# Sharing the first head's 32-block inverse between VectorE and GpSimd, and asking for it three slots earlier

## The chip, the cores and the metric

The kernel runs on one core of one Trainium2 chip. The metric is the device time of one launch in microseconds (us), the median of several runs. Before the change three runs gave 2298.82, 2300.39 and 2301.43 us, median 2300.39 us.

## The reference

A decoder trunk of two layers over 1024 tokens of width 1024. Layer 0 is a gated DeltaNet with 8 heads (key width 128, value width 256), layer 1 a dilated sliding-window attention. Each layer is an RMS norm, one input projection, the mixer, a gate, an output projection and a residual add. The part that matters here is the triangular solve of the delta rule:

```
lower = where(strict, einsum("bhnid,bhnjd->bhnij", k_beta, k) * decay, 0.0)
rhs   = concatenate([v * beta, k_beta * exp(g)], axis=-1)
sol   = triangular_solve(lower + eye(C), rhs, left_side=True, lower=True, unit_diagonal=True)
```

The kernel solves it by inverting unit lower triangular matrices, for 8 tiles of 128 tokens in each head.

## The kernel before, in words

Everything is one program with five instruction queues (TensorE = PE, VectorE = DVE, ScalarE = ACT, GpSimd = POOL, SyncE = SP), each in program order, tied together by counting semaphores. There is no scheduler: the order on each queue is written out by hand in **slots**. One head of the delta layer has 36 slots (0 to 35) and trails of up to 42. In every slot TensorE does 8 matmuls of 128x512 of the input projection (`three_passes`, L383): 6 weight units of 128 columns a head, each in two halves of 512 tokens, a half q = 0..11 in slots 3q to 3q+2. Weights are split in a high and a low part, so a half takes 24 matmuls. Around these matmuls stand the other steps of the head, each in a fixed slot.

`body(m, n, p)` writes one round: it projects head n and, beside it, runs the delta recurrence of the head before, m. The first round has no m. So the first head's inverse is made in the round `body(None, 0, 0)` and used in the next, `body(0, 1, 1)`, from slot 4 on.

**The inverse.** The tiles u (the strictly lower matrices) are written to DRAM in slot 16 (L658) and their 32x32 diagonal blocks come back as `bd`, one block a partition spread over four partition groups (L663). Each group q of 32 partitions computes 8 of the 32 columns of the inverse of its blocks: `bx` is 128 partitions x 32 rows x 8 columns. GpSimd does a forward substitution in 31 steps: step j multiplies column j of `bd` below the diagonal by row j of `bx` (L766, into `bt`) and subtracts the product from the rows below (L769). Each of the 62 instructions waits on a semaphore for the one before. At last a copy turns `bx` (L774, into `bxt`, which lies in `bd`).

**The way back.** In slot 33 (INVERSE_BACK) the SP queue waits for that copy, stores four parts of `bx` and four of the turned copy (L711, L712), waits for them, and issues four loads into `zx` (L716). TensorE reads `zx` in slot 4 of the next round (L1112), from which two levels build the 128-inverse (L1112, ScalarE's copy L823, L1117 and L1119).

**Weights.** In every slot s with s mod 6 = 3 the SP queue issues one weight load of 512 KB (L620; unit j = s//6 + 1, and in slot 33 unit 0 of the next head), once its buffer is free, which is when VectorE's low part of the unit before the last is done (`wa_w_low`). ScalarE makes the high part (L786) one slot ahead of VectorE's low part (L1128). The two buffers alternate. In the code, slot 33's weight load stands ahead of slot 33's inverse wait.

**Evacuation and gates.** ScalarE copies each finished half out of PSUM in slot 3q+3 (L864 for q below 8, L872 for the last four) and runs three passes for its sigmoid in slot 3q+5 (L877, L879, L881). VectorE does the four taps of the convolution and the sigmoid's argument in slot 3q+4 (L1258, L1260, L1266) and the product with the sigmoid in slot 3q+6 (L1273, or L1277 for the gate halves). TensorE's half q in slot 3q waits until ScalarE has evacuated half q-2. TensorE turns the value halves 4 to 7 in slots 20, 23, 26 and 29 (L1057), for which it waits until VectorE has made them (L1273), and multiplies keys with queries in slots 21 and 24 (L1091); the second of these waits for VectorE's use of the first (L1299). The keys are turned in slots 32 and 35 (L1049).

Of the kernel before, what the change touches and what calls it, by code (L numbers as in the profile page):

```python
# [22 lines left out]
ALU = mybir.AluOpType  # L23
# [21 lines left out]
BLK = 32  # L45
NB = P // BLK
LEVELS = 2
PARTS_OF_BLOCK = P // BLK
PART = BLK // PARTS_OF_BLOCK
# [11 lines left out]
def spread(ap, axis, n):  # L61

    v = ap.unsqueeze(axis)
    shape = list(v.shape)
    shape[axis] = n
    return v.broadcast_to(shape)


class Mem:
# [11 lines left out]
    def sem(self, name):  # L81
        return self.ctx.enter_context(self.nc.semaphore(f"{self.tag}_{name}"))
# [278 lines left out]
Q_GRAMS = (21, 24)  # L361
BLOCKS_OUT = 16
INVERSE_BACK = 33
DELAYED = SLOTS + 6
OUT_RING = 8
OUT_TILES = A_VW // P
# [59 lines left out]
def delta_heads(nc, g, weights, proj, o_turned, front, o_stored, early):  # L426
# [5 lines left out]
    with ExitStack() as ctx:  # L432
# [17 lines left out]
        cols = m_.sb("cols", [P, 7, T, H])  # L450
        hc = m_.sb("hc", [P, 2, 6, T])
        hw = m_.sb("hw", [P, 2, CONV, 4])
        bd = m_.sb("bd", [P, BLK, BLK])
        bx = m_.sb("bx", [P, BLK, PART])
# [7 lines left out]
        r = m_.sb("r", [P, DV])  # L462
# [8 lines left out]
        rows = m_.sb("rows", [4 * H, HALF], F32R)  # L471
# [33 lines left out]
        sem = m_.sem  # L505
# [12 lines left out]
        blocks_out, blocks_in, blocks_inv = sem("blocks_out"), sem("blocks_in"), sem("blocks_inv")  # L518
        inv_out, inv_zero = sem("inv_out"), sem("inv_zero")
        back = [sem("back_first"), sem("back_rest")]  # L520
        bstep = sem("bstep")
        zx_zero = sem("zx_zero")
        um_s, first_mm, first_c, lv_mm, lv_s = (sem(x) for x in ("um", "first_mm", "first_c", "lv_mm", "lv_s"))
        ks_mm, r_s, xr_mm, vn_s = sem("ks_mm"), sem("r_s"), sem("xr_mm"), sem("vn_s")
# [90 lines left out]
        def _(sp):  # L615
# [21 lines left out]
            def body(m, n, p):  # L637
                for s in range(DELAYED):
                    if n is not None and s < SLOTS and s % 6 == 3:
                        j = s // 6 + 1  # L640
# [60 lines left out]
                    if m is not None and (s - CHAIN0 - 8) % 3 == 0 and 0 <= (s - CHAIN0 - 8) // 3 < T:  # L701
                        t = (s - CHAIN0 - 8) // 3
                        sp.wait_ge(og_s, m * T + (t + 1 + T))
                        dst = o_turned[bass.ds(m * DV, DV), t * P:(t + 1) * P].rearrange("(c p) n -> p c n", p=P)
                        sp.dma_start(dst, og[:, :, :]).then_inc(o_stored, 16)
                    if n is not None and s == INVERSE_BACK:
                        sp.wait_ge(blocks_inv, n * 2 + 2)

                        sp.wait_ge(lv_s, n * (LEVELS * T // 2) + 1)
                        for q in range(PARTS_OF_BLOCK):  # L710
                            sp.dma_start(as_blocks(inv_dram[1])[:, :, columns(q)], part_of(bx, q)).then_inc(inv_out, 16)  # L711
                            sp.dma_start(as_blocks(inv_dram[0])[:, columns(q)], part_of(bxt, q)).then_inc(inv_out, 16)  # L712
                        sp.wait_ge(inv_out, (n + 1) * (32 * PARTS_OF_BLOCK))
                        for part, tiles in enumerate((slice(0, 2), slice(2, T))):
                            for c in range(2):
                                sp.dma_start(zx[:, tiles, c, :], as_tiles(inv_dram[c])[:, tiles]  # L716
                                             ).then_inc(back[part], 16)
# [3 lines left out]
        @block.gpsimd  # L721
        def _(pool):
            pool.memset(zx[:, :, :, :], 0.0).then_inc(zx_zero, 1)
            pool.wait_ge(cols_s, 1)

            def body(m, n, p):
                if n is not None:
                    columns_and_taps(n, p)
                if m is not None:
                    for b in range(T // 2):  # L730

                        pool.wait_ge(first_mm, m * (LEVELS * T // 2) + (LEVELS * max(b - 1, 0) + 1))
                        pool.wait_ge(ut, m * 4 + 2)
                        pool.tensor_tensor(um[:, b % 2], spread(u[:, 2 * b:2 * b + 2, :], 2, LEVELS),  # L734
                                           spread(g.level_mask[:, :, :], 1, 2), ALU.mult).then_inc(um_s, 1)
                if n is not None:
                    invert_blocks(n)

            def columns_and_taps(n, p):

                pool.wait_ge(og_s, n * T)
                pool.tensor_copy(hc[:, p], cols[:, 0:C_LOG, :, bass.ds(n, 1)].rearrange("p a t o -> p a (t o)")
                                 ).then_inc(hc_s, 1)
                pool.tensor_copy(pick[:, p, :], cols[0:4 * H, C_LOG, 0:2, bass.ds(n, 1)].rearrange("r a o -> r (a o)")
                                 ).then_inc(hc_s, 1)
                for c, tile in ((0, n + H), (1, n + 0), (2, n * 2 + 2 * H), (3, n * 2 + (2 * H + 1))):
                    pool.tensor_copy(hw[:, p, :, c:c + 1], g.conv[:, :, bass.ds(tile, 1)]).then_inc(hc_s, 1)

            def invert_blocks(n):

                if not (isinstance(n, int) and n == 0):
                    pool.wait_ge(inv_out, n * (32 * PARTS_OF_BLOCK))
                pool.sem_inc(carrier, 1)
                pool.memset(bx[:, :, :], 0.0).then_inc(bstep, 1)
                pool.wait_ge(bstep, n * (2 * BLK) + 1)
                pool.sem_inc(carrier, 1)
                for q in range(PARTS_OF_BLOCK):
                    diag = part_of(bx, q)[:, columns(q), :].rearrange("t i c -> t (i c)")[:, 0:PART * PART:PART + 1]
                    ins = pool.tensor_copy(diag, part_of(g.ones, q)[:, 0:PART])
                ins.then_inc(bstep, 1)  # L760
                pool.wait_ge(blocks_in, (n + 1) * (16 * PARTS_OF_BLOCK))
                for j in range(BLK - 1):
                    pool.wait_ge(bstep, n * (2 * BLK) + (2 + 2 * j))
                    rows, width = BLK - 1 - j, min(j + 1, PART)
                    prod = bt[:, 0:rows * width].rearrange("t (i c) -> t i c", c=width)
                    pool.tensor_tensor(prod, spread(bd[:, j, j + 1:BLK], 2, width),  # L766
                                       spread(bx[:, j, 0:width], 1, rows), ALU.mult).then_inc(bstep, 1)
                    pool.wait_ge(bstep, n * (2 * BLK) + (3 + 2 * j))
                    pool.tensor_tensor(bx[:, j + 1:BLK, 0:width], bx[:, j + 1:BLK, 0:width], prod,  # L769
                                       ALU.subtract).then_inc(bstep if j < BLK - 2 else blocks_inv, 1)  # L770

                pool.wait_ge(blocks_inv, n * 2 + 1)
                pool.sem_inc(carrier, 1)
                pool.tensor_copy(bxt, bx[:, :, :].rearrange("t i c -> t c i")).then_inc(blocks_inv, 1)  # L774
                pool.wait_ge(blocks_inv, n * 2 + 2)
                pool.sem_inc(bstep, 1)

            heads(pool, body)
# [346 lines left out]
        def _(dve):  # L1125
# [50 lines left out]
            def next_weight(n, s):  # L1176
                j = s // 6 + 1
                if j < UNITS or n < H - 1:
                    split_low(n * UNITS + (1 + j), slot_of(j % UNITS))

            def body(m, n, p):
                pm = 1 - p
                for s in range(DELAYED):
                    if m is not None:
                        b, k = divmod(s - LEVEL0 - 2, LEVEL_STEP)
                        if 0 <= b < T // 2 and k in range(0, 2 * LEVELS, 2) and not (n is not None and s == CHAIN0 + 1):
                            merge(m, b, k // 2)
                        t, k = divmod(s - CHAIN0, 3)
# [19 lines left out]
                        t, k = divmod(s - CHAIN0 - 6, 3)  # L1208
# [5 lines left out]
                    if n is not None:  # L1214
                        if s - 1 in K_GRAMS:
# [7 lines left out]
                            for e in range(TH):  # L1223
                                t = half * TH + e
# [44 lines left out]
                        if 0 <= q < HALVES and k == 0:  # L1269
# [4 lines left out]
                            else:  # L1274
                                c = q // 2 - 4
# [1267 lines left out]
```

## Time and profile before

| | us |
|---|---|
| three runs | 2298.82, 2300.39, 2301.43 |
| the profiled execution's own time | 2299.51 |
| its span, first to last instruction | 2297.8 |
| PE busy | 2243.4 (98%) |
| DVE busy | 1400.1 (61%) |
| ACT busy | 1229.9 (54%) |
| POOL busy | 400.2 (17%) |

Times in the rows are microseconds from the span's start. The first head's round runs from about 44 to 123 us: the turn of its last keys in slot 35 starts at 122.95 us, and the first matmul of the second head's slot 0 at 123.31 us. An instruction's row gives its start, its duration, engine, line, operation, tiles and shapes, and in brackets how long its engine sat idle before it and what released it.

### The profile page before, as it was taken

The numbers are of one execution on the slowest core, as the hardware profiler recorded it, in microseconds if no ns is written. First come the engines' busy times: TensorE is split into PE (matmuls) and PEld (weight loads), VectorE is DVE, ScalarE is ACT, GpSimd is POOL, SyncE is SP. The second block draws the span as 40 slices with busy tenths as digits, with TensorE's granted clock in tenths as the row PEclk, the third lists the DMA queues.
The fourth block names the chain that finished last, engine by engine and source line by source line (L and its number), as shares of the span: only waits on it lengthen the run. The fifth ranks groups of instructions, "written<-read, shape, count | busy, mean of one in ns | idle before, by whom it ended". The sixth has DMA issues, their size and how long they took to land. (4 is left out here: it accounts for less than half of the span.)

```text
span 2297.8 us, 31341 instructions
## 1 busy us (share of the span) xinstructions
PE 2243.4 (98%) x11056; PEld 1873.0 (82%) x11056; DVE 1400.1 (61%) x2594; ACT 1229.9 (54%) x2509; POOL 400.2 (17%) x672
## 2 busy tenths in 40 slices
PE   7989999999999999999999999999999999999989
PEld 5778888887888888787888888888888888888877
DVE  5756767585767665586745728365482745738341
ACT  5646566666666665555545455454554545455430
POOL 1435161533425160560000000000000000000000
PEclk9999999999999999999999999999999999999999
DMA  4222232313222245585111121121111211121151
GB/s 142 46 53 62 63 88 51 81 41 75 49 67 60 58 104 179 183 273 192 56 38 56 28 59 44 38 65 38 47 37 47 65 38 56 28 56 47 54 217 51
DMA packets 301727, 174.26 MB, mean 76 GB/s; under 512 B 97229, under 2 KB 284005, under 8 KB 301573
## 3 DMA queue, kind: packets, MB, share of 16 engines
q1 hardware_dynamic: 301572, 172.26, 26.3%
q8 instruction: 90, 1.47, 0.3%
q14 instruction: 65, 0.52, 0.1%
HBM read 143.66 MB, written 28.56 MB: 75 GB/s over the span
## 5 line engine op out<-in xcount | busy, mean ns | idle before, releaser
L383 PE MATMUL b_front<-g_h_hi,wa_w_hi 128*128 128x512 f32 x2064 | 822.5, 398 | 4.7 <-PEq L1503 3.0
L383 PE MATMUL b_front<-g_h_lo,wa_w_hi 128*128 128x512 f32 x2064 | 827.0, 401 | 0.0
L383 PE MATMUL b_front<-g_h_hi,wa_w_lo 128*128 128x512 f32 x2064 | 823.4, 399 | 0.0
L383 PEld LDWEIGHTS b_front<-g_h_hi,wa_w_hi 128*128 128x128 f32 x2064 | 389.1, 189 | 81.5 <-issue 5.5
L383 PEld LDWEIGHTS b_front<-g_h_lo,wa_w_hi 128*128 128x128 f32 x2064 | 388.9, 188 | 77.1 <-issue 0.2
L383 PEld LDWEIGHTS b_front<-g_h_hi,wa_w_lo 128*128 128x128 f32 x2064 | 388.6, 188 | 76.1 <-issue 0.5
L2154 ACT ACTIVATE b_acc<-b_front,g_gains 128x512 f32<-128x512 f32 x96 | 66.1, 689 | 301.7 <-DVE b_qk L2458 211.2
L1260 DVE SCALAR_TENSOR_TENSOR a_acc<-a_x_raw,a_hw,a_acc 128x512 f32<-128x512 f32 x192 | 156.9, 817 | 6.8
L2332 DVE TENSOR_TENSOR wa_w_lo<-wa_raw,wa_w_hi 128x1024 fp32r<-128x1024 f32 x79 | 95.6, 1210 | 106.0 <-ACT wa_w_hi L2100 106.0
L766 POOL TENSOR_TENSOR a_bt<-a_bd,a_bx 128x112 f32<-128x112 f32 (+29 forms) x248 | 117.3, 473 | 214.8 <-DMA a_bd<-u_tiles 196.0
L769 POOL TENSOR_TENSOR a_bx<-a_bx,a_bt 128x112 f32<-128x112 f32 (+29 forms) x248 | 130.6, 527 | 19.4
L2423 DVE TENSOR_TENSOR b_sq_lo<-b_sg,b_sq_hi 128x512 fp32r<-128x512 f32 x96 | 66.3, 690 | 89.4 <-ACT b_sq_hi L2159 89.4
L877 ACT ACTIVATE a_sg<-a_sg 128x512 f32<-128x512 f32 x96 | 60.0, 625 | 78.6 <-DVE a_sg L1266 78.6
L2458 DVE TENSOR_TENSOR b_qk<-b_acc,b_sg 128x512 f32<-128x512 f32 x96 | 90.2, 939 | 0.0
L2187 ACT ACTIVATE b_v<-b_side 128x512 f32<-128x512 f32 x48 | 28.6, 595 | 106.8 <-PE b_side L2315 106.8
L2015 DVE COPY b_kept<-b_ring 128x512 f32<-128x512 f32 (+1 forms) x28 | 18.3, 653 | 107.3 <-PE b_ring L2264 107.3
L2100 ACT ACTIVATE wa_w_hi<-wa_raw 128x1024 fp32r<-128x1024 f32 x79 | 82.7, 1047 | 0.0
L734 POOL TENSOR_TENSOR a_um<-a_u,g_level_mask 128x512 f32<-128x512 f32 x32 | 42.2, 1327 | 229.4 <-PE a_lev L1112 229.2
L2166 ACT ACTIVATE b_v_raw<-b_front 128x512 f32<-128x512 f32 x48 | 28.6, 595 | 90.6 <-PE b_front L383 90.6
L2243 PE MATMUL b_ring<-b_qk 128*128 128x128 f32 (+1 forms) x384 | 76.6, 322 | 0.0
L830 ACT ACTIVATE a_o<-a_step,a_hc 128x256 f32<-128x256 f32 x56 | 26.6, 475 | 90.9 <-DVE a_r L1191 90.9
L1128 DVE TENSOR_TENSOR wa_w_lo<-wa_raw,wa_w_hi 128x1024 fp32r<-128x1024 f32 x47 | 58.4, 1243 | 23.4 <-ACT wa_w_hi L786 23.4
(343 smaller groups left out, 4087.0 us busy)
## 6 DMA issues: line engine op xcount, KB each, us to landing
wa_raw<-in_b_w_in_dram SPq DMA_DIRECT2D x80, 512.0 KB, 3.9
wa_raw<-in_a_w_in_dram SPq DMA_DIRECT2D x48, 512.0 KB, 4.3
p_w_raw<-in_a_w_out_dram SPq DMA_DIRECT2D x40, 512.0 KB, 3.9
a_out<-a_og SPq DMA_DIRECT2D x64, 128.0 KB, 1.9
a_zx<-inverse_tiles SPq DMA_DIRECT2D x16, 384.0 KB, 4.5
p_a_raw<-a_out SPq DMA_DIRECT2D x40, 128.0 KB, 5.0
u_tiles<-a_u SPq DMA_DIRECT2D x8, 512.0 KB, 3.2
a_bd<-u_tiles SPq DMA_DIRECT2D x32, 128.0 KB, 3.7
```

What stands on the lines that cost most here:

```text
L383: last = pe.matmul(out, w[:, k, :], a[:, k, ks], start=(n == 0), stop=(n == 23))
L766: pool.tensor_tensor(prod, spread(bd[:, j, j + 1:BLK], 2, width), spread(bx[:, j, 0:width], 1, rows), ALU.mult).then_inc(bstep, 1)
L769: pool.tensor_tensor(bx[:, j + 1:BLK, 0:width], bx[:, j + 1:BLK, 0:width], prod, ALU.subtract).then_inc(bstep if j < BLK - 2 else blocks_i ...
L877: act.activation(sg[:, q % 2], sg[:, q % 2], ACT.Exp).then_inc(sigs, 1)
L1128: dve.tensor_tensor(w_lo[slot][:, :, :], raw[:, slot], w_hi[slot][:, :, :].bitcast(F32), ALU.subtract).then_inc(w_low, 1)
L1260: ins = dve.scalar_tensor_tensor(acc[:, half], src, w, acc[:, half], ALU.mult, ALU.add)
L2100: act.activation(w_hi[slot_of(j)][:, :, :], raw[:, slot_of(j)], ACT.Copy).then_inc(w_high, 1)
L2154: act.activation(acc[:, half], proj[half][:, :], ACT.Copy, scale=r.gains[:, gain:gain + 1]).then_inc(rope, 1)
L2243: mm = pe.matmul(ring[i % 3][:, c * 2 * P:c * 2 * P + width], qk[:, 2 * g, first:first + P], qk[:, 2 * g + 1, begin:begin + width], start= ...
L2332: dve.tensor_tensor(w_lo[slot_of(j)][:, :, :], raw[:, slot_of(j)], w_hi[slot_of(j)][:, :, :].bitcast(F32), ALU.subtract).then_inc(w_low, 1)
L2423: dve.tensor_tensor(sq_lo[:, :], sg[:, q % 2], sq_hi[:, :].bitcast(F32), ALU.subtract).then_inc(sq_low, 1)
L2458: dve.tensor_tensor(out, a, b_, ALU.mult).then_inc(qkn, 1)
```

## The change

Three edits, all of them for the first head only (n = 0).

1. GpSimd's 31 steps work on columns 0 to 3 of each part (width 4 in place of 8).
2. VectorE does columns 4 to 7: 27 steps (j = 4 to 30) of two instructions, three steps at the head of each of the slots 20 to 28, with a semaphore of their own (`shared`), each instruction waiting for the one before. They use `r` as the place of the product. The columns don't depend on each other, so neither engine waits for the other's steps; GpSimd's copy L774 now waits for both.
3. The SP queue waits for the inverse and sends it to DRAM and back in slot 30 in place of 33.

```diff
+FIRST_BACK = 30
+SHARED = PART // 2
+SHARED_STEPS = {20 + i: range(SHARED + 3 * i, min(SHARED + 3 * i + 3, BLK - 1)) for i in range(9)}
...
-                    if n is not None and s == INVERSE_BACK:
+                    if n is not None and s == (INVERSE_BACK if n else FIRST_BACK):
...
-                    rows, width = BLK - 1 - j, min(j + 1, PART)
+                    rows, width = BLK - 1 - j, min(j + 1, PART if n else SHARED)
...
+                if n == 0:
+                    pool.wait_ge(shared, 2 * (BLK - 1 - SHARED))
...
+            def invert_columns(steps):
+
+                for j in steps:
+                    done = 2 * (j - SHARED)
+                    if j == SHARED:
+                        dve.wait_ge(bstep, 2)
+                        dve.wait_ge(blocks_in, 16 * PARTS_OF_BLOCK)
+                    else:
+                        dve.wait_ge(shared, done)
+                    rows, width = BLK - 1 - j, min(j + 1, PART) - SHARED
+                    cols = slice(SHARED, SHARED + width)
+                    prod = r[:, 0:rows * width].rearrange("t (i c) -> t i c", c=width)
+                    dve.tensor_tensor(prod, spread(bd[:, j, j + 1:BLK], 2, width), spread(bx[:, j, cols], 1, rows),
+                                      ALU.mult).then_inc(shared, 1)
+                    dve.wait_ge(shared, done + 1)
+                    dve.tensor_tensor(bx[:, j + 1:BLK, cols], bx[:, j + 1:BLK, cols], prod, ALU.subtract
+                                      ).then_inc(shared, 1)
+
             def body(m, n, p):
                 pm = 1 - p
                 for s in range(DELAYED):
+                    if m is None and s in SHARED_STEPS:
+                        invert_columns(SHARED_STEPS[s])
```

The diff doesn't show what edit 3 moves on the SP queue, because slots 30 and 33 lie in one loop. This is the queue of the kernel before, from the load of the blocks `bd` on; the three weight loads in its second row are units 4 and 5 of the first head (slots 21 and 27) and unit 0 of the second (slot 33).

```order
L663 DMA a_bd<-u_tiles 32x32x32 x4
L620 DMA wa_raw<-in_a_w_in_dram 128x8x128 x3
L711 DMA inverse_tiles<-a_bx 32x32x8
L712 DMA inverse_tiles<-a_bd 32x8x32
L711 DMA inverse_tiles<-a_bx 32x32x8
L712 DMA inverse_tiles<-a_bd 32x8x32
L711 DMA inverse_tiles<-a_bx 32x32x8
L712 DMA inverse_tiles<-a_bd 32x8x32
L711 DMA inverse_tiles<-a_bx 32x32x8
L712 DMA inverse_tiles<-a_bd 32x8x32
L716 DMA a_zx<-inverse_tiles 128x2x128 x2
L716 DMA a_zx<-inverse_tiles 128x6x128 x2
```

Behind these rows the queue goes on with L620 x3. And this is the same place in the changed kernel, where the lines have moved by 3.

```order
L666 DMA a_bd<-u_tiles 32x32x32 x4
L623 DMA wa_raw<-in_a_w_in_dram 128x8x128 x2
L714 DMA inverse_tiles<-a_bx 32x32x8
L715 DMA inverse_tiles<-a_bd 32x8x32
L714 DMA inverse_tiles<-a_bx 32x32x8
L715 DMA inverse_tiles<-a_bd 32x8x32
L714 DMA inverse_tiles<-a_bx 32x32x8
L715 DMA inverse_tiles<-a_bd 32x8x32
L714 DMA inverse_tiles<-a_bx 32x32x8
L715 DMA inverse_tiles<-a_bd 32x8x32
L719 DMA a_zx<-inverse_tiles 128x2x128 x2
L719 DMA a_zx<-inverse_tiles 128x6x128 x2
```

Two weight loads stand ahead of the wait where three stood, and L623 x4 follow in place of three: the second head's unit 0 has changed sides.

On VectorE, this is what stands from the sigmoid's argument of half 5 (slot 19) to the convolution of half 6 (slot 22) in the kernel before.

```order
L1266 TENSOR_SCALAR a_sg<-a_acc 128x512 [waits a_convs]
L1128 TENSOR_TENSOR wa_w_lo<-wa_raw,wa_w_hi 128x1024 [waits wa_w_high]
L1273 TENSOR_TENSOR a_acc<-a_acc,a_sg 128x512 [waits a_sig]
L1258 TENSOR_SCALAR a_acc<-a_x_raw,a_hw 128x512 [waits a_v_turned,a_evac,a_act_out]
L1260 SCALAR_TENSOR_TENSOR a_acc<-a_x_raw,a_hw,a_acc 128x512 [waits a_taps] x3
```

In the changed kernel 12 new instructions stand ahead of the weight's low part (slots 20 and 21; the last two of them are shown) and 6 ahead of the convolution (slot 22).

```order
L1198 TENSOR_TENSOR a_r<-a_bd,a_bx 128x88 [waits a_shared]
L1201 TENSOR_TENSOR a_bx<-a_bx,a_r 128x22x4 [waits a_shared]
L1133 TENSOR_TENSOR wa_w_lo<-wa_raw,wa_w_hi 128x1024 [waits wa_w_high]
L1298 TENSOR_TENSOR a_acc<-a_acc,a_sg 128x512 [waits a_sig]
L1198 TENSOR_TENSOR a_r<-a_bd,a_bx 128x84 [waits a_shared]
L1201 TENSOR_TENSOR a_bx<-a_bx,a_r 128x21x4 [waits a_shared]
L1198 TENSOR_TENSOR a_r<-a_bd,a_bx 128x80 [waits a_shared]
L1201 TENSOR_TENSOR a_bx<-a_bx,a_r 128x20x4 [waits a_shared]
L1198 TENSOR_TENSOR a_r<-a_bd,a_bx 128x76 [waits a_shared]
L1201 TENSOR_TENSOR a_bx<-a_bx,a_r 128x19x4 [waits a_shared]
L1283 TENSOR_SCALAR a_acc<-a_x_raw,a_hw 128x512 [waits a_v_turned,a_evac,a_act_out]
```

The same goes on up to slot 28, 54 new instructions in all, with every older instruction in its old order.

## Rows read from the trace of the kernel before

**Rows 1.** The page, part 1: busy time of each engine.
```profile
PE 2243.4 (98%) x11056; PEld 1873.0 (82%) x11056; DVE 1400.1 (61%) x2594; ACT 1229.9 (54%) x2509; POOL 400.2 (17%) x672
```

**Rows 2.** TensorE's waits from 40 to 200 us: engine, line, releaser, total, times, longest.
```profile
PE a_lev L1117 <- ACT a_bc L823: 4.5, 1, 4.5
...
PE a_lev L1112 <- issue: 1.7, 1, 1.7
```

**Rows 3.** TensorE in order of time, 123 to 145 us.
```profile
123.31 0.48 PE L383 MATMUL b_front<-g_h_hi,wa_w_hi 128*128 128x512 f32 x1
...
134.33 0.68 PE L1112 MATMUL a_lev<-a_zx,a_um 128*128 128x128 f32 x4 [1.68 <-issue]
...
141.31 0.80 PE L1117 MATMUL a_lev<-a_zx,a_bc 128*128 128x128 f32 x2 [4.45 <-ACT a_bc L823]
...
143.04 0.78 PE L383 MATMUL b_front<-g_h_hi,wa_w_hi 128*128 128x512 f32 x1
```

**Rows 4.** ScalarE in order of time.
```profile
112.80 1.06 ACT L786 ACTIVATE wa_w_hi<-wa_raw 128x1024 fp32r<-128x1024 f32 x1
...
117.24 0.60 ACT L872 ACTIVATE a_acc<-b_front 128x512 f32<-128x512 f32 x1 [1.54 <-PE b_front L383]
120.69 0.63 ACT L877 ACTIVATE a_sg<-a_sg 128x512 f32<-128x512 f32 x1 [2.85 <-DVE a_sg L1266]
...
139.44 1.06 ACT L786 ACTIVATE wa_w_hi<-wa_raw 128x1024 fp32r<-128x1024 f32 x1 [12.17 <-DMA wa_raw<-in_a_w_in_dram]
140.41 0.58 ACT L864 ACTIVATE a_x_raw<-b_front 128x512 f32<-128x512 f32 x1
```

**Rows 5.** The SP queue: its wait for the inverse, then its DMAs in time.
```profile
SPq L711 <- POOL a_bd L774: 31.2, 1, 31.2
...
94.25 0.37 SPq L620 DMA_DIRECT2D wa_raw<-in_a_w_in_dram  x1
...
133.58 2.17 SPq L620 DMA_DIRECT2D wa_raw<-in_a_w_in_dram  x2
```

**Rows 6.** Granted clock and busy times, 140 to 145 us.
```profile
140.00:145.00 5.00, 3.69 (x14) 3.31 (x14) 4.33 (x7) 1.26 (x3) 0.00 (x0) 0.66 0.42 113
```

**Rows 7.** GpSimd in order of time: first and last steps and some between.
```profile
87.77 0.24 POOL L766 TENSOR_TENSOR a_bt<-a_bd,a_bx 128x31 f32<-128x31 f32 x1 [34.90 <-DMA a_bd<-u_tiles]
...
93.16 1.32 POOL L769 TENSOR_TENSOR a_bx<-a_bx,a_bt 128x135 f32<-128x135 f32 x1
...
111.35 0.39 POOL L766 TENSOR_TENSOR a_bt<-a_bd,a_bx 128x120 f32<-128x120 f32 x1
111.82 0.44 POOL L769 TENSOR_TENSOR a_bx<-a_bx,a_bt 128x120 f32<-128x120 f32 x1
...
124.14 0.20 POOL L766 TENSOR_TENSOR a_bt<-a_bd,a_bx 128x8 f32<-128x8 f32 x1
...
125.17 0.67 POOL L774 COPY a_bd<-a_bx 128x256 f32<-128x256 f32 x1 [0.17 <-POOL a_bx L769]
```

**Rows 8.** Stretches: length, then busy (x) of PE, PEld, DVE, ACT, POOL; clock, DMA.
```profile
92.70:109.90 17.20, 17.20 (x89) 14.54 (x88) 14.77 (x19) 9.56 (x16) 15.55 (x22) 1.00 0.11 30
```

**Rows 9.** VectorE in order of time: the weight's low part; the first tap alone, then beside GpSimd.
```profile
89.38 0.49 DVE L1258 TENSOR_SCALAR a_acc<-a_x_raw,a_hw 128x512 f32<-128x512 f32 x1
...
92.72 1.44 DVE L1128 TENSOR_TENSOR wa_w_lo<-wa_raw,wa_w_hi 128x1024 fp32r<-128x1024 f32 x1
...
95.50 0.73 DVE L1258 TENSOR_SCALAR a_acc<-a_x_raw,a_hw 128x512 f32<-128x512 f32 x1
```

**Rows 10.** VectorE's groups by shape: mean ns of one; idle before, over the count.
```profile
L2365 DVE TENSOR_TENSOR b_mo<-b_mo,b_mx 128x8 f32<-128x8 f32 x8 | 1.3, 168 | 0.3
L2438 DVE TENSOR_TENSOR b_acc<-b_acc,t_cos 32x512 f32<-32x512 f32 x96 | 64.6, 673 | 0.0
```

**Rows 11.** TensorE's last turn of values (slot 29).
```profile
111.13 0.60 PE L1057 MATMUL a_turn<-g_ident,a_acc 128*128 128x128 f32 x4
```

**Rows 12.** The weight loads L620, 80 to 200 us: time from issue to landing.
```profile
DMA to landing us min/median/max: 4.0/5.8/6.9
```

More of the change, by code:

```diff
@@ L520, in delta_heads @@
         back = [sem("back_first"), sem("back_rest")]
-        bstep = sem("bstep")
+        bstep, shared = sem("bstep"), sem("shared")
         zx_zero = sem("zx_zero")
```

## The prediction

> **What bounds the kernel now.** I read the busy times first: TensorE is busy 98% of the span, no other engine more than 61% [rows 1]. An edit to VectorE and GpSimd can win only where TensorE stands still, so I went to TensorE's waits around the first head. Between 40 and 200 us there are two that hang on the inverse [rows 2], and the timeline shows where. In slot 4 of the second head L1112 stands idle 1.68 us for `zx`; one slot on, L1117 stands idle 4.45 us for ScalarE's copy L823 [rows 3]. Together 6.1 us.
>
> The first ends right after `zx` begins to land. The second isn't a wait for the inverse itself. ScalarE stood 12.17 us for a weight load before 139.44 (unit 1 of the second head), and L823 is queued behind that [rows 4]. The SP queue says why the load was late: SP waited 31.2 us for GpSimd's copy L774, sent the inverse away and back, and only at 133.58 issued the weight [rows 5]. So both stalls are one: the inverse ends at 125.84 (125.17 + 0.67) [rows 7], and everything behind SP's wait is late. A last cost is the clock: in 140 to 145 us the granted clock is 0.66 [rows 6], a mix of 2.4 and 1.2 GHz, after those 4.45 us idle.
>
> **Edit 1, GpSimd on half the columns.** With no collision, 120 elements take 0.39 us in the multiplication and 0.44 in the subtraction, 8 elements 0.20, and the next one starts 0.08 us behind the end of the one before [rows 7]. That is 0.19 us fixed and 0.08 idle for each instruction, 0.54 us a step, and 1.7 + 2.1 = 3.8 ns an element for the pair. The 31 steps had 2964 elements an instruction (31, 60, 87, 112, 135, 156, 175, then 8 x 24 down to 8 x 1) and get 1802 (31, 60, 87, then 4 x 28 down to 4 x 1). Undisturbed, 31 x 0.54 + 2964 x 0.0038 = 28.0 us becomes 23.6 us. Real were 37.2 us (87.77 to 125.0): 9.2 us are lost beside VectorE. One row shows how: the subtraction at 93.16 took 1.32 us while VectorE's 1024-element subtraction ran from 92.72 to 94.16, and that one took 1.44 [rows 7, 9]. Most of this loss stays, since VectorE's old instructions all stay in the stretch; I take 7.5 us. GpSimd then ends at 87.8 + 23.6 + 7.5 = 118.9 at the earliest, and the new small VectorE instructions come on top, perhaps 1 to 4 us.
>
> **Edit 2, VectorE does the other half.** 54 instructions, each waiting for the one before. No such instruction is in this place yet; the nearest are 128x8 at 168 ns with about 0.04 us idle between, and a two-input 512 one at 673 ns [rows 10], so 0.16 us + 1.01 ns an element, + 0.04. Elements are 27, 52, 75, then 4 x 24 down to 4 x 1: 1354, twice 2708. Sum: 54 x 0.20 + 2708 x 0.00101 = 13.5 us. The low end is 54 x 0.205 = 11.1 us, the elements free. For the high end each has to wait for a GpSimd instruction, as the first tap did that took 0.73 us beside GpSimd and 0.49 alone [rows 9]: 54 x 0.24 = 13 more, 26.5 us. GpSimd's instructions will be short, so I add 0.03 us each: 15.1 us.
>
> What cover is there? From 92.7 to 109.9 us VectorE is busy 14.8 of 17.2 us [rows 8]; only 2.4 us are free, and six sevenths of the new work doesn't fit. VectorE becomes the bound of this stretch. Counted out: it has 14.2 us of old work between 92.7 and its instruction behind the last new one (14.8 less the 0.6 of that instruction itself), so the last new step ends at 92.7 + 14.2 + 15.1 = 122.0. GpSimd, at 120 to 123, is close beside. The copy L774 adds 0.15 + 0.67: the inverse is ready at about **122.8** instead of 125.84, 3.0 us earlier, not 15.
>
> On the way TensorE is held. Slot 24's product waits for L1299, which comes behind 18 new instructions (about 5.5 us), and slot 29's turn of half 7 comes behind L1273, now past the steps of slots 20 to 27. That L1273 ends at about 120.6 us (122.0 less the last block's 1.4), where the turn stood at 111.13 [rows 11]. So TensorE is about 9.5 us late at slot 30. That alone would bring its slot 36 (slot 0 of the second head) from 123.31 to 132.8. It is hidden only because something still later follows.
>
> **Edit 3, the wait moved to slot 30.** It is moved past one DMA: the load of the second head's unit 0, which before was issued at 94.25 and whose high part ScalarE made at 112.80 with no wait [rows 4, 5]. Now it is issued after the inverse's trip. From L774's end to the next weight load that trip took 133.58 - 125.84 = 7.74 us; the weight issued there was waited for until 139.44, 5.86 us [rows 4, 5]. Behind ScalarE's wait for it are queued, in order: L786 itself (0.97 us to the next start), three passes of half 9's sigmoid (0.63 each, 1.96 with the gaps), and the evacuation of half 10 (0.60) [rows 4], for which TensorE's slot 36 waits. Sum 7.74 + 5.86 + 0.97 + 1.96 + 0.60 = 17.1 us. Slot 36 therefore starts at 122.8 + 17.1 = **139.9**, where it started at 123.31: 16.6 us late, and 7.1 us behind even the held TensorE.
>
> Then the gains. `zx` is there at about 131.3 (122.8 + 8.5, the time from 125.84 to the row of L1112), and unit 1's weight was issued with unit 0's: both old stalls go, 6.1 us. The restart after the 4.45 us cost (1 - 0.66) x 5 = 1.7 us [rows 6]; I count 1.0 of it before 143.04, an estimate, since the group from 141.31 to 143.04 took 1.73 us [rows 3] and is twice that of L1112 (0.68 with its tail), and 0.7 after it. Slots 36 to 41 (123.31 to 143.04) are then 19.7 - 6.1 - 1.0 = 12.6 us of work. A restart after 7 us idle pays the 1.7 again. So slot 42 begins at 139.9 + 12.6 + 1.7 = 154.2, against 143.04 + 0.7 = 143.7 before: **+10.5 us**. As a formula, the shift is the inverse's end less 112.3 us. Behind it TensorE is the bound as before, nothing gives the time back, and the other heads are unchanged.
>
> The profiled execution took 2299.51 us, 0.88 below the median of the runs. Added to the median: 2300.4 + 10.5 = **2310.9 us**.
>
> A rule of the Trainium skill speaks against this change harder than I do. SBUF — State Buffer, section "Who interferes with whom", says that a VectorE instruction with two SBUF inputs and a GpSimd instruction that reads SBUF exclude each other, and the loser is blocked until the other ends. The 1.32 us row agrees with it; the result it would give is the first rival.
>
> **Rivals.**
> *The two engines take turns.* Each of the 54 instructions waits for a running GpSimd one and the other way round. For it: 0.49 to 0.73 us, and the 1.32 us. Against it: GpSimd's waits are for long VectorE instructions, and its own are 0.2 to 0.4 us. Priced: 5 to 11 us more, inverse at 128 to 134, +16 to +22 us, about 2319.
>
> *Little changes.* The inverse comes early, at about 120, and the landing is short: the fastest of these loads land after 4.0 us [rows 12], 1.9 less, and the clock doesn't fall. +7.7 - 1.9 - 1.7 = +4.1 us, 2304.5. For it, the low bound of the new instructions.
>
> *Faster, the intended way.* The steps of both engines are done by slot 28 or 29 and the unit 0 load isn't late. It decides at an inverse's end of 112.3; full gain is below 106.2, where slot 36 starts at 123.3 and slot 42 at 135.9, 7.8 us off at most. Against it: GpSimd even undisturbed ends at 87.8 + 23.6 + 0.8 = 112.2, and VectorE would need its 15 us in 2.4. With the short landing and no slow clock that gives -0.1 - 3.6 = -3.7, 2296.7.
>
> *The change doesn't do what it says*, that is VectorE's steps wait for GpSimd's: excluded, they wait only for the blocks and the first two GpSimd steps, done long before.
>
> **How the numbers follow.** Forecast (inverse at 119 to 127, +7 to +15) 0.68; taking turns 0.18; little change 0.09; faster 0.05. One comparison of this kernel can tell 0.2%, 4.6 us. Faster by more 0.05, within 0.08, slower 0.87. The range goes from 2304.5, the little change's own time, to 2320, which takes in half of taking turns. That leaves out about 0.18: 0.05 for faster, 0.04 of the little change, 0.09 of taking turns.
>
> **What would show it.** In the changed profile: the 54 small instructions with a mean of 0.21 to 0.25 us and starts 0.26 to 0.31 us apart; L1299's successor late by 5 us; TensorE idle before the turn of slot 29 (4 to 6 us) and again before slot 0 of the second head (about 7 us, released by ScalarE's evacuation); ScalarE idle over 10 us before the high part of unit 0; the SP's wait for the copy ending near 123; no wait at L1117. I am wrong if the copy ends before 115, or if slot 36 starts before 132.

## The result: 0.44% slower, and the profile after

| | before | changed |
|---|---|---|
| median of 6 runs each, us | 2300.89 | 2310.85 |
| lowest to highest | 2298.82 to 2301.82 | 2308.34 to 2313.78 |
| ratio, 95% interval | | 1.0044, 1.0034 to 1.0054 |
| profiled execution, span | 2299.51, 2297.8 | 2311.55, 2309.8 |

The change costs 10.0 us. 2310.9 was forecast.

One thing has to be set aside before rows are compared. The delta layer's first matmul starts at 36.77 us in this profile and at 34.74 in that of before. Over all the profiled executions below, it starts anywhere from 34.3 to 37.0. So I take 2.03 us off a time of the changed kernel to set it beside one of before ("in before's time"). For a whole run's shift in a profile I take a **marker**: the start of the first `a_new<-a_v_front` matmul (slot 8 of the second head, the first place at which all kernels do the same work again) less the start of the delta layer's first matmul. It is 117.31 us in the profile of before.

The page's first part, against [rows 1]: VectorE has 54 instructions and 13.8 us more, GpSimd 8.3 us less.

```profile
PE 2248.8 (97%) x11056; PEld 1876.4 (81%) x11056; DVE 1413.9 (61%) x2648; ACT 1229.6 (53%) x2509; POOL 391.9 (17%) x672
```

TensorE's waits from 40 to 200 us in the changed kernel, against [rows 2] (engine, line, releaser, total, times, longest):

```profile
PE b_front L386 <- ACT a_acc L877: 5.9, 1, 5.9
...
PE b_front L1096 <- DVE a_attn L1324: 3.8, 1, 3.8
PE a_turn L1062 <- DVE a_acc L1298: 3.2, 2, 2.1
...
PE a_new L982 <- issue: 0.5, 1, 0.5
```

Both old stalls (4.45 and 1.68 us) are gone. In their place stand three that [rows 2] don't have: 3.8 and 3.2 us for VectorE, and 5.9 us for ScalarE's evacuation of half 10. TensorE in order of time shows where they lie, up to slot 42 (the row at 156.56):

```profile
101.62 0.66 PE L1062 MATMUL a_turn<-g_ident,a_acc 128*128 128x128 f32 x4 [1.10 <-DVE a_acc L1298]
...
107.90 1.13 PE L1096 MATMUL b_front<-a_kq 128*128 128x128 f32 x8 [3.77 <-DVE a_attn L1324]
...
122.30 0.79 PE L1062 MATMUL a_turn<-g_ident,a_acc 128*128 128x128 f32 x4 [2.08 <-DVE a_acc L1298]
...
142.24 0.76 PE L386 MATMUL b_front<-g_h_hi,wa_w_hi 128*128 128x512 f32 x1 [5.89 <-ACT a_acc L877]
...
156.56 0.48 PE L386 MATMUL b_front<-g_h_hi,wa_w_hi 128*128 128x512 f32 x1
```

The SP queue and then ScalarE of the changed kernel, against [rows 4, 5]. The first weight load behind the inverse is now issued at 132.81, and ScalarE's high part of unit 0 waits 12.09 us for it; in the kernel before it had no wait.

```profile
124.20 0.33 SPq L714 DMA_DIRECT2D inverse_tiles<-a_bx  x1
...
127.87 1.33 SPq L715 DMA_DIRECT2D inverse_tiles<-a_bd  x1
130.70 1.99 SPq L719 DMA_DIRECT2D a_zx<-inverse_tiles  x4
132.81 2.30 SPq L623 DMA_DIRECT2D wa_raw<-in_a_w_in_dram  x2
```

```profile
138.71 1.06 ACT L791 ACTIVATE wa_w_hi<-wa_raw 128x1024 fp32r<-128x1024 f32 x1 [12.09 <-DMA wa_raw<-in_a_w_in_dram]
139.67 0.61 ACT L882 ACTIVATE a_sg<-a_sg 128x512 f32<-128x512 f32 x1
...
141.52 0.58 ACT L877 ACTIVATE a_acc<-b_front 128x512 f32<-128x512 f32 x1
```

Some of GpSimd's steps, the last one and its copy, and then the 54 new VectorE instructions grouped over 92 to 125 us (mean ns of one, then the idle time before them):

```profile
97.45 0.35 POOL L769 TENSOR_TENSOR a_bt<-a_bd,a_bx 128x96 f32<-128x96 f32 x1
...
99.63 1.39 POOL L772 TENSOR_TENSOR a_bx<-a_bx,a_bt 128x88 f32<-128x88 f32 x1
...
119.64 0.20 POOL L772 TENSOR_TENSOR a_bx<-a_bx,a_bt 128x4 f32<-128x4 f32 x1
123.48 0.69 POOL L779 COPY a_bd<-a_bx 128x256 f32<-128x256 f32 x1 [3.63 <-DVE a_bx L1201]
```

```profile
L1198 DVE TENSOR_TENSOR a_r<-a_bd,a_bx 128x52 f32<-128x52 f32 (+25 forms) x27 | 7.9, 291 | 0.7
...
L1201 DVE TENSOR_TENSOR a_bx<-a_bx,a_r 128x52 f32<-128x52 f32 (+25 forms) x27 | 7.6, 282 | 0.9
```

GpSimd's steps were done at 119.84 and its copy then stood 3.63 us for VectorE's last step. The inverse ends at 124.17, in before's time 122.1, against 125.84 before.

### The profile page after: what moved, and what is told of

Read it like the earlier page. It is cut to its first block and busy times, and to the rows that moved or that the text cites. A ratio compares the mean times of both kernels' runs of the same rounds, so it can differ in the third digit from the quotient of the medians.

```text
span 2309.8 us, 31396 instructions
## 1 busy us (share of the span) xinstructions
PE 2248.8 (97%) x11056; PEld 1876.4 (81%) x11056; DVE 1413.9 (61%) x2648; ACT 1229.6 (53%) x2509; POOL 391.9 (17%) x672
## 5 line engine op out<-in xcount | busy, mean ns | idle before, releaser
L386 PEld LDWEIGHTS b_front<-g_h_lo,wa_w_hi 128*128 128x128 f32 x2064 | 390.7, 189 | 77.6 <-issue 0.2
L769 POOL TENSOR_TENSOR a_bt<-a_bd,a_bx 128x112 f32<-128x112 f32 (+35 forms) x248 | 111.1, 448 | 213.4 <-DMA a_bd<-u_tiles 194.5
L772 POOL TENSOR_TENSOR a_bx<-a_bx,a_bt 128x112 f32<-128x112 f32 (+35 forms) x248 | 129.4, 522 | 19.4
L2448 DVE TENSOR_TENSOR b_sq_lo<-b_sg,b_sq_hi 128x512 fp32r<-128x512 f32 x96 | 66.3, 690 | 89.8 <-ACT b_sq_hi L2184 89.7
```

The source lines that it names most:

```text
L386: last = pe.matmul(out, w[:, k, :], a[:, k, ks], start=(n == 0), stop=(n == 23))
L2448: dve.tensor_tensor(sq_lo[:, :], sg[:, q % 2], sq_hi[:, :].bitcast(F32), ALU.subtract).then_inc(sq_low, 1)
```

## The experiments

Eleven runs, in three sets (e1 to e4, e5 to e8, e9 to e11), each set timed in the same rounds as the kernel before: medians 2300.38, 2301.28 and 2299.96 us. The interval behind a ratio is its 95%.

### Each edit alone

**e1_back_only**: the kernel before with the wait moved, nothing else.

```diff
-                    if n is not None and s == INVERSE_BACK:
+                    if n is not None and s == (INVERSE_BACK if n else FIRST_BACK):
```

> Edit 3 alone: the SP queue waits for the first head's inverse in slot 30, GpSimd does all 8 columns as before. Theory A (the load of the second head's unit 0, now behind the inverse's trip, sets the end): the inverse ends where it did, about 125.8, ScalarE's high part of unit 0 starts near 139.5, TensorE's slot 0 of the second head starts at 125.8 + 17.1 = 142.9 after an idle of some 19 us, and the kernel is 13 us slower than before (between 11 and 15). Theory B (the rival: the loss in the changed kernel comes from VectorE's 54 new instructions, and the order on the SP queue is hidden): within 3 us of before.

Measured: 2311.99 us, +11.6, ratio 1.0050 (1.0037 to 1.0062); marker +11.9. Inside the 11 to 15 expected. The queue alone costs more than the whole change. TensorE waits in one piece at slot 0 of the second head:

```profile
142.50 0.77 PE L384 MATMUL b_front<-g_h_hi,wa_w_hi 128*128 128x512 f32 x1 [18.06 <-ACT a_acc L873]
```

**e2_share_only**: edits 1 and 2, the wait stays in slot 33 (`FIRST_BACK = 33`).

> Edits 1 and 2 without edit 3: the columns are shared, the SP queue waits in slot 33 as before, so unit 0's weight is loaded early. Theory A: TensorE is held about 9 us by VectorE (slots 24 and 29), both old stalls of the second head's slots 4 and 5 go, and the kernel is 1 to 4 us slower than before, 7 us or more faster than with all three edits. Theory B (VectorE's new instructions carry the loss): about 10 us slower than before, as with all three edits.

Measured: 2300.76 us, +0.4, ratio 1.0000 (0.9991 to 1.0009); marker +0.6. That is under the 1 to 4 us expected, and far from theory B's 10: the sharing itself costs nothing that can be measured, and gains nothing. TensorE's waits from 40 to 200 us:

```profile
PE b_front L1096 <- DVE a_attn L1324: 3.8, 1, 3.8
PE a_turn L1062 <- DVE a_acc L1298: 3.3, 2, 2.2
...
PE a_new L982 <- issue: 0.5, 1, 0.5
```

The hold by VectorE is there as in the changed kernel (7.1 us of idle time with 1.1 us in slot 23), and the 6.1 us of the old stalls and the slow clock behind them are gone. One was paid with the other.

### The stretch with the wait in slot 30: when must the inverse end?

**e6_half_gpsimd_back_early**: the wait in slot 30, GpSimd with 4 columns, no VectorE steps, so that nobody computes the other columns; **e10_half_again** is the same kernel in the third set. **e9_quarter_gpsimd_back_early**: 2 columns in place of 4.

```diff
-                    rows, width = BLK - 1 - j, min(j + 1, PART)
+                    rows, width = BLK - 1 - j, min(j + 1, PART if n else PART // 2)
```

> GpSimd does columns 0 to 3 alone (4 to 7 are left undone), no step on VectorE, and the SP queue waits in slot 30. The run with the wait in slot 33 had its inverse at 122.2 us, with the round 1.1 us late from the start, so 121.1. Theory A (the chain inverse, trip, unit 0's weight, ScalarE, slot 0 sets the end, and VectorE's hold is hidden under it): 121.1 - 112.3 = 8.8 us slower than before, between 7 and 10.5, within 2 us of the changed kernel. Rival (VectorE's hold of TensorE is a part of the changed kernel's 10 us): 5 us slower than before or less.

Measured: 2306.36 us, +5.1, ratio 1.0022 (1.0012 to 1.0032); marker +7.0. Under the range of 7 to 10.5 by its median, though the profiled execution (2309.82 us, +8.5) is inside. Taken alone this would leave the rival standing; e10 below repeats it.

**e7_vector_steps_alone**: the changed kernel, GpSimd without its steps for the first head (it only counts up the semaphores that they would have counted up); VectorE's stay.

```diff
-                for j in range(BLK - 1):
+                for j in range(BLK - 1 if n else 0):
```

> The changed kernel without GpSimd's 31 steps for the first head (columns 0 to 3 stay as they were set, nobody computes them): VectorE's 54 instructions run with nothing beside them on GpSimd. Theory A (in the changed kernel they took 17.2 us from start to start because the two engines hold each other up): they take 13 to 14 us here, the large ones 0.25 to 0.30 us in place of 0.35 to 0.47; the inverse ends about 3.6 us earlier and the kernel is 6 to 7 us slower than before. Rival (their length is their own, from the strided operands): 17 us again, and about 10 us slower than before.

Measured: 2308.31 us, +7.0, ratio 1.0028 (1.0017 to 1.0038); marker +6.6. The 54 instructions take 12.5 us from start to start where the changed kernel takes 16.65. The groups of e7, and the 96-element multiplication, whose row in the changed kernel (beside GpSimd's) stands behind it:

```profile
L1205 DVE TENSOR_TENSOR a_bx<-a_bx,a_r 128x52 f32<-128x52 f32 (+25 forms) x27 | 5.7, 212 | 0.9
...
L1202 DVE TENSOR_TENSOR a_r<-a_bd,a_bx 128x52 f32<-128x52 f32 (+25 forms) x27 | 5.7, 210 | 0.7
...
96.32 0.26 DVE L1202 TENSOR_TENSOR a_r<-a_bd,a_bx 128x96 f32<-128x96 f32 x1
```

```profile
97.02 0.47 DVE L1198 TENSOR_TENSOR a_r<-a_bd,a_bx 128x96 f32<-128x96 f32 x1
```

> GpSimd does columns 0 and 1 of each part for the first head (2 to 7 are left undone), no step on VectorE, the wait for the inverse in slot 30. 961 elements an instruction give 20.4 us undisturbed, + 7.5 to 8.5 us lost beside VectorE + 0.8: the inverse ends near 117 in the time of the kernel before. Theory A (the kernel's end follows the inverse's end one for one, with 112.3 as the point of no change): +4.7 us, between 3 and 6.5, and 3 to 4 us less than with half the columns. Rival (something after slot 0 takes up the difference): the same time as with half the columns.

Measured: 2303.16 us, +3.2, ratio 1.0015 (1.0006 to 1.0024); marker +3.9. Inside the 3 to 6.5 expected.

> Columns 0 to 3 on GpSimd alone (4 to 7 left undone), wait in slot 30, a second time and beside the changed kernel. The first time it was 5.1 us slower than before by the clock (interval 2.8 to 7.4), while its profiled execution had slot 0 of the second head 14.4 us late, which stands for +8 to +9. Theory A: it takes 1 to 3 us less than the changed kernel in the same rounds, and 7 to 9 us more than before. Rival (VectorE's hold costs something of its own): 4 us or more less than the changed kernel.

Measured: 2307.36 us, +7.4, ratio 1.0034 (1.0022 to 1.0047); marker +6.5. It is 3.6 us under the changed kernel's second run (e11), and 4.1 by the markers, where 1 to 3 were expected and the rival asked for 4 or more. The traces give the rival nothing: of the 4.1 us, 2.8 are the earlier end of the inverse and 1.4 a shorter way from there to slot 36 (table below).

**e11_changed_again**: the changed kernel in the third set.

> The changed kernel itself, for comparison in the same rounds: 10 us slower than before.

Measured: 2310.92 us, +11.0, ratio 1.0049 (1.0037 to 1.0062); marker +10.6. TensorE's start of slot 36:

```profile
142.81 0.77 PE L386 MATMUL b_front<-g_h_hi,wa_w_hi 128*128 128x512 f32 x1 [7.77 <-ACT a_acc L877]
```

This and the first profile of the changed kernel are two executions of one program, and they show that the hold by VectorE is hidden. Here TensorE was ready for slot 36 at 132.8 in before's time, in the first at 134.3 (there its clock had fallen behind slot 29); it stood idle 7.77 us here and 5.89 there, and the marker is no earlier for it (+10.6 against +10.2).

Seven profiles now have the wait in slot 30. Their inverse's end (less the start of the delta layer) and their marker's shift:

| kernel | inverse's end, us | marker, us | inverse's end to slot 36, us |
|---|---|---|---|
| e9, 2 columns | 82.5 | +3.9 | 17.0 |
| e7, VectorE's steps alone | 83.1 | +6.6 | 18.4 |
| e10, e6, 4 columns | 84.7, 85.0 | +6.5, +7.0 | 17.0, 17.9 |
| changed, e11 | 87.4, 87.5 | +10.2, +10.6 | 18.1, 18.4 |
| e1, 8 columns | 89.8 | +11.9 | 17.1 |

From e9 to e1 the inverse ends 7.3 us later and the marker shifts by 8.1: close to one for one. The forecast's formula gives the inverse's end less 77.6 us here (112.3 less the 34.7 at which the delta layer starts), that is +4.9 for e9, +5.5 for e7, +9.8 for the changed kernel and +12.2 for e1; all seven lie within 1.1 us of it. What is left goes mostly with the last column. In that column 17.0 and 17.1 us stand where the last of the eight stores took 0.56 us to issue (e9, e10, e1), and 18.1 to 18.4 where it took longer: 1.33 us in the changed kernel, 1.35 in e11, and in e7

```profile
123.73 1.79 SPq L715 DMA_DIRECT2D inverse_tiles<-a_bd  x1
```

e6 is the exception: its last store took 0.56 us, and its 17.9 us come from unit 0's weight, for which ScalarE's high part started 6.67 us behind the issue, against 5.73 in e10.

By this table, which engine does the columns makes no difference beyond the time at which they end, within the 1.1 us. And with a quarter of the columns and nothing on VectorE the inverse still ends 5 us behind the forecast's point of no change.

### Was the old 4.45 us stall a late weight?

**e3_half_gpsimd**: the kernel before, GpSimd with 4 columns (nobody computes the others), the wait in slot 33.

> GpSimd does columns 0 to 3 of each part for the first head, and columns 4 to 7 are left undone (nobody computes them); the SP queue waits in slot 33. Theory A: the inverse ends at about 119.7 (23.6 us undisturbed + 7.5 lost beside VectorE + 0.8), zx is there at 128.2, the weight of unit 1 is issued at 127.4; both stalls (1.7 and 4.5 us) and the slow clock behind them go, 6 to 8 us faster than before. Rival: GpSimd loses less beside VectorE because its instructions are short, the inverse ends at 115 or earlier; the time is then the same, since the stalls are gone either way. It is slower or the same only if the stalls of slots 4 and 5 hang on something else than the inverse.

Measured: 2295.84 us, -4.5, ratio 0.9980 (0.9971 to 0.9989); marker -4.2. Less than the 6 to 8 expected, because the inverse ended later than I had worked out, at 121.1 in before's time and not 119.7: GpSimd's 31 steps took 32.4 us. So unit 1's weight was still late, and 1.6 us were left at L1117. Two other waits, behind it, took back a part too: 0.9 us at the next L1112, and 2.2 us at L977 where the kernel before had 1.0. ScalarE's wait for unit 1's weight, and TensorE's waits:

```profile
135.87 1.06 ACT L786 ACTIVATE wa_w_hi<-wa_raw 128x1024 fp32r<-128x1024 f32 x1 [7.21 <-DMA wa_raw<-in_a_w_in_dram]
```

```profile
PE a_new L977 <- issue: 2.2, 1, 2.2
PE a_lev L1117 <- ACT a_bc L823: 1.6, 1, 1.6
PE a_lev L1112 <- DVE a_zx L1171: 0.9, 1, 0.9
```

**e4_weights_first**: the kernel before, and units 1 and 2 of the second head are loaded in slot 33 too, ahead of the wait. Nothing else moves.

```diff
-                            load(n, j)
+                            if n != 1 or j > 2:
+                                load(n, j)
...
+                            if n == 0:
+                                load(1, 1)
+                                load(1, 2)
```

> The kernel before, with one thing moved on the SP queue: the second head's weight units 1 and 2 are issued in slot 33 ahead of the wait for the inverse, not behind it. GpSimd does all 8 columns. Theory A (the 4.45 us stall at L1117 is a late weight load, not the inverse): unit 1 is issued near 108 us, ScalarE doesn't wait 12 us for it, the stall at L1117 and the slow clock behind it go, the 1.7 us wait for zx stays: 5 to 6 us faster than before. Rival (ScalarE's copy L823 is late because of the inverse itself): no more than 1 us faster.

Measured: 2293.38 us, -7.0, ratio 0.9966 (0.9954 to 0.9979); marker -4.6. Two DMA issues moved, and the kernel is faster than the kernel before and the changed one. ScalarE's high part of unit 1 has no wait left, and of TensorE's two old stalls only that for `zx` is there:

```profile
127.52 1.04 ACT L790 ACTIVATE wa_w_hi<-wa_raw 128x1024 fp32r<-128x1024 f32 x1
```

```profile
PE a_lev L1116 <- issue: 2.5, 1, 2.5
...
PE a_new L981 <- issue: 0.5, 1, 0.5
```

The wait for `zx` has grown from 1.7 to 2.5 us, and the slow clock, which was expected to go, is still there behind it (the first row below; the second is e8). The marker's 4.6 us are under the 5 to 6 expected, the medians' 7.0 over it, with an interval of 4.8 to 10.6 us. So the trace around the first head accounts for 4.6 us, and where the rest stands isn't known.

```profile
135.00:140.00 5.00, 4.53 (x18) 3.94 (x19) 0.00 (x0) 2.62 (x5) 0.00 (x0) 0.66 0.90 247
```

```profile
135.00:140.00 5.00, 4.51 (x26) 3.99 (x27) 2.50 (x5) 2.73 (x5) 0.00 (x0) 1.00 0.95 258
```

**e5_share_weights_first**: edits 1 and 2 with the wait in slot 33, and e4's loads.

> Columns shared, the SP queue waits in slot 33, and the second head's weight units 1 and 2 stand ahead of the wait. Theory A (sharing trades the inverse's stalls for TensorE held about 9 us by VectorE, and with the weights out of the way there is nothing left to win by it): as the sharing alone with its +0.4 us, so -1 to +1.5 us against before, and 6 to 8 us slower than the weights moved without sharing. Rival (sharing and moved weights add up): 7 us or more faster than before.

Measured: 2299.73 us, -1.6 by the medians, ratio 0.9998 (0.9990 to 1.0007); marker +2.2. The 7 us of e4 are not had on top of the sharing: what e4 takes away, the held TensorE has hidden already. Here the moved loads have a price of their own. Unit 2's load waits for its buffer until 130.06, so the inverse, ready at 121.80, is sent away only at 130.53, 8.7 us later; TensorE doesn't wait for `zx` even so, since it comes to slot 4 only at 142.96.

**e8_weights_first_store_early**: e4, and the four stores of `bx` go out before GpSimd's copy; only the stores of the turned copy wait for it.

```diff
-                        sp.wait_ge(blocks_inv, n * 2 + 2)
+                        sp.wait_ge(blocks_inv, n * 2 + (1 if n == 0 else 2))
...
+                            for q in range(PARTS_OF_BLOCK):
+                                sp.dma_start(as_blocks(inv_dram[1])[:, :, columns(q)], part_of(bx, q)).then_inc(inv_out, 16)
+                            sp.wait_ge(blocks_inv, 2)
+                            for q in range(PARTS_OF_BLOCK):
+                                sp.dma_start(as_blocks(inv_dram[0])[:, columns(q)], part_of(bxt, q)).then_inc(inv_out, 16)
```

> The kernel with the weight units 1 and 2 ahead of the wait, all 8 columns on GpSimd, and for the first head the four stores of bx issued before GpSimd's copy (they wait only for the last subtraction), the four stores of the copy after it. The wait of TensorE in slot 4 for zx was 2.5 us in the run before. Expected: the trip starts 0.8 us earlier, the wait falls to 1.7 us, 0.8 us faster than the run before, so 7.8 us faster than before. Rival: the trip is bound by the eight stores' landing and not by their issue; no change to 7.0 us.

Measured: 2292.66 us, ratio 0.9965 (0.9951 to 0.9978), so -8.1 by the ratio and -8.6 by the medians; marker -7.5. The fastest of all, though not told apart from e4 by its interval. Expected were 7.8. The wait for `zx` is down from e4's 2.5 us to 1.0, more than the 0.8 expected: from the end of GpSimd's copy to the issue of `zx`'s load it takes 4.64 us, in e4 5.93. And with the shorter wait the granted clock didn't fall (the second row above), so the marker gains 2.9 us on e4 and not 0.8.

```profile
PE a_lev L1123 <- issue: 1.0, 1, 1.0
PE a_new L988 <- issue: 0.5, 1, 0.5
```

## Why the prediction was right, point by point

**The bound, and what the old stalls were.** Held. e4 is the proof: without a word about the inverse, the 4.45 us at L1117 go when unit 1's load stands ahead of the wait.

**Edit 1.** GpSimd was to end at 120 to 123 by the cautious count, 118.9 at the earliest. It ended at 117.8 in before's time: 30.1 us for the steps, 23.6 undisturbed, so the loss was 6.5 and not 7.5 or more. A slip stands in the count: the 31 steps of the kernel before have 3156 elements an instruction, not 2964, so undisturbed they would take 28.7 us and the loss beside VectorE was 8.5, not 9.2. The 1802 of the half are right. None of it mattered, since VectorE was last (the copy's 3.63 us).

**Edit 2.** Two terms were off and cancelled, which is luck. The 54 instructions took 16.65 us, not 15.1: means of 291 and 282 ns, where 210 to 250 stood in the forecast. The forecast's 13.5 us undisturbed were 12.5 in e7, so the collision is worth 4.1 us and not 1.6. On the other hand VectorE's old work took 12.0 us of the stretch (28.62 us from the first new instruction's start at 94.70 to the end of the last at 123.32, less 16.65), not 14.2. VectorE's long instructions in the changed kernel run like undisturbed ones:

```profile
99.58 1.21 DVE L1133 TENSOR_TENSOR wa_w_lo<-wa_raw,wa_w_hi 128x1024 fp32r<-128x1024 f32 x1
...
104.36 2.33 DVE L1285 SCALAR_TENSOR_TENSOR a_acc<-a_x_raw,a_hw,a_acc 128x512 f32<-128x512 f32 x3
```

In the kernel before the same two took 1.44 us [rows 9] and 2.72 us (the three taps at 96.26). GpSimd's instructions are half as long now, and it is they that are held (99.63), no longer VectorE's long ones; in e3, with the half steps and no new VectorE instructions, the taps take 2.38 and 2.33 us too. The forecast carried the old work over at its stretched length. The inverse was ready at 122.1 against 122.8, by errors of +1.6 and -2.2 us.

**TensorE held.** 122.30 is 120.27 in before's time, 9.14 us behind [rows 11]; 9.5 was forecast. But its make-up was not what I said would be seen: 4 to 6 us idle at slot 29's turn. The idle time there is 2.08 us, with 3.77 at slot 24 and 1.10 at slot 23, 6.95 together; the rest, 2.2 us, goes with the lower clock. In e11 the turn is 9.19 us behind [rows 11], with less idle time (6.25 us) and a lower clock (0.63 and 0.69 in 105 to 115): it is VectorE that sets when the turn can start. The granted clock, in stretches of the changed kernel (length, then busy (x) of PE, PEld, DVE, ACT, POOL; clock, DMA):

```profile
100.00:105.00 5.00, 3.03 (x15) 1.92 (x13) 4.79 (x10) 0.00 (x0) 4.37 (x9) 1.00 0.00 0
105.00:110.00 5.00, 2.10 (x11) 1.85 (x12) 4.69 (x12) 2.75 (x5) 4.14 (x11) 0.90 0.00 2
110.00:115.00 5.00, 5.00 (x20) 4.05 (x19) 4.62 (x14) 1.06 (x2) 4.06 (x13) 0.76 0.00 0
...
140.00:145.00 5.00, 2.76 (x7) 2.21 (x8) 2.96 (x5) 4.21 (x8) 0.00 (x0) 0.50 0.39 105
145.00:150.00 5.00, 5.00 (x20) 4.04 (x19) 2.78 (x4) 3.05 (x5) 0.00 (x0) 0.84 0.00 0
```

VectorE is busy 4.7 of each 5 us there: it is the bound of the stretch, as forecast.

**Edit 3**, the step that decides. Forecast 17.1 us from the inverse to slot 36, measured 18.07. The trip took 132.81 - 124.17 = 8.64 us instead of 7.74: one of the store issues took 1.33 us, the others on the same line 0.56. The landing took 5.90 (5.86), ScalarE's chain 3.53 (3.53). Slot 36 began at 142.24, in before's time 140.2; forecast 139.9. The 1.0 us too little here met the 0.7 us too much in the inverse's end. e1 shows that this step alone gives the slowdown, and the table of seven profiles that the shift hangs on the inverse's end.

**The gains and slot 42.** 156.56 is 154.5 in before's time, forecast 154.2. No wait is left at L1117 or its neighbour. The restart after 5.89 us of idle time cost what was counted: 9 matmuls 0.43 us apart (142.24 to 146.22) instead of 0.23, some 1.9 us, with the granted clock at 0.50 in 140 to 145, the lower of the two levels. The idle time itself was to be about 7 us; TensorE had lost 1.5 us more on its way than forecast, with the granted clock at 0.77 in 120 to 125 and 0.89 in 125 to 130. Behind slot 42 the changed kernel gets back 1.3 us against the 0.7 forecast: 0.5 of it is the wait at `a_new` (0.99 us before, 0.48 now), a term that the sum didn't have. So the sum's errors, -0.7 (inverse), +1.0 (way to slot 36) and -0.6 (behind slot 42), nearly cancel: +10.2 by the marker against +10.5.

**The rivals.** "Taking turns" is partly true: the engines do fall in step around the longest of the new instructions, but it costs 4.1 us in all, 1.6 more than forecast and not 5 to 11. The 1.32 us instruction of [rows 7] has its like in the changed kernel (99.63, 1.39 us for 88 elements), and that one is GpSimd's. "Little change" needed the inverse at 120 and a landing of 4.0 us; neither came. "Faster" needed an end by 112.3; it came at 122.1, and with a quarter of the columns and no VectorE steps at all (e9) it is still +3.2 us.

The Trainium skill's rule (SBUF — State Buffer, "Who interferes with whom") is agreed with by the direction of e7 against the changed kernel: two-input VectorE instructions of 96 elements take 0.26 us alone and 0.47 beside GpSimd. Full exclusion at every instruction, by which the rival was priced, isn't seen: around 97 to 99 us both chains start an instruction every 0.42 to 0.50 us, less than the 0.61 us that VectorE's 0.26 and GpSimd's 0.35 add up to.

**Where the time went.** The change brings the inverse 3.7 us forward and takes away both stalls (6.1 us). Against it stand two delays of slot 36: TensorE, held by VectorE, is ready for it 11.0 us later than before (9.5 in e11), and the evacuation that hangs on unit 0's load comes 5.9 us (7.8) behind even that, 16.9 us late (17.3). Only the later of the two sets the end.

**Still open.** e6 and e10 are one kernel and gave +5.1 and +7.4 us, with intervals of 2.8 to 7.4 and 5.1 to 10.8 us; they overlap, but the sets may also differ. Why the last store's issue takes 0.56 us in one execution and 1.33 or 1.79 in another is not known. Whether the last 1.5 us of waits in e8 can go wasn't tried.

## What to carry to other kernels

In a DMA queue that is served in order, look at what is queued behind a wait before looking at what is waited for: 3 slots earlier for the wait cost 11.6 us here, and two loads moved ahead of it brought 7.0 (4.6 by the marker), while halving the work that is waited for brought 4.5. Before work is split over a second engine, read how much that engine is idle in the very stretch (2.4 of 17.2 us here, and not the 39% of the whole span). Two remedies for the same stall don't add up: the sharing and the moved loads each took the stall at L1117 away, and together (e5) they gave no more than the sharing alone, since the hold that the sharing brings stayed.

## What the runs showed of the hardware that was not expected

- After about 2 us of idle time TensorE's granted clock fell in one execution and not in another. Two kernels that hold TensorE in the same places (2.1 and 2.2 us idle before slot 29's turn), e5 (idle until 119.92) and then e2 (idle until 121.99), TensorE's busy time and granted clock around the end of the idle time:

```profile
120.00:125.00 5.00, 5.00 (x17) 0.66 0.39 105
```

```profile
120.00:125.00 5.00, 3.01 (x15) 1.00 0.03 2
125.00:130.00 5.00, 5.00 (x25) 1.00 0.53 52
```

- GpSimd's half steps took no longer beside VectorE's small steps (30.1 us in the changed kernel, 30.2 in e11) than without them (32.4 us in e3, 31.1 in e6, 30.8 in e10). Beside the small ones GpSimd's are undisturbed (96 elements in 0.35 us at 97.45); the ones that are held run beside VectorE's long ones (1.39 us at 99.63).
- The start of the delta layer scatters by 2.7 us between executions, and the kernel before's own times from 2296.6 to 2305.0 in one set: differences under 2 us need a marker inside the trace, and even that scattered by 1 to 2 us.
